# Moving taps, norms and z tiles around the triangular inverse of a gated DeltaNet layer on one core

## The reference, cut to what matters

```python
qkv = jax.nn.silu(causal_depthwise_conv(h[..., Q0:Z0], conv_w))    # 4 taps; q, k, v
q = l2_normalize(qkv[:, :, 0]) * (GDN_HEAD_DIM ** -0.5)
...
a_mat = jnp.where(strict, jnp.einsum('bhncd,bhnsd->bhncs', kb, k) * decay, 0.0)
sol = lax.linalg.triangular_solve(a_mat, rhs, left_side=True, lower=True, unit_diagonal=True)
u, w = sol[..., :Dv], sol[..., Dv:]
qk = jnp.einsum('bhncd,bhnsd->bhncs', q, k) * decay
...
v_new = uc - jnp.einsum('bhcd,bhde->bhce', wc, S)                  # in a scan over the chunks
o = jnp.einsum('bhcd,bhde->bhce', qd, S) + jnp.einsum('bhcs,bhse->bhce', qkc, v_new)
S = S * eg[..., None, None] + jnp.einsum('bhcd,bhce->bhde', kd, v_new)
...
o = o * jax.nn.silu(z)
```

## Time and profile before

| | us |
|---|---|
| median of 3 runs | 2034.25 (2034.21 to 2036.57) |
| profiled execution | 2035.76 |
| its span | 2034.0 |
| TensorE busy | 2009.4 (99%) |
| VectorE busy | 1157.3 (57%) |
| ScalarE busy | 782.3 (38%) |
| mean granted TensorE clock | 0.997 |

### The profile page before, as it was taken

One profiled execution on the slowest core, in us unless ns is written; L12 is line 12 of the kernel. 1 busy time (PEld: TensorE's weight loads), 2 busy tenths in 40 slices (PEclk: granted clock), 3 DMA queues, 4 the chain that ended last, 5 costly groups with the idle time before them and its releaser, 6 DMA issues.

```text
span 2034.0 us, 25396 instructions
## 1 busy us (share of the span) xinstructions
PE 2009.4 (99%) x9637; PEld 1677.9 (82%) x9637; DVE 1157.3 (57%) x1622; ACT 782.3 (38%) x1199; POOL 40.8 (2%) x68
## 2 busy tenths in 40 slices
PE   9999999999999999999999999999999999999998
PEld 7888888878988888888888888888879888888886
DVE  5554532699785755442285545237998766554324
ACT  5222222457765422222252222225586653222223
POOL 1000000011000000000000000000110000000000
PEclk9999999999999999999999999999999999999999
DMA  6333333276222333333323333333761224333331
GB/s 168 113 89 102 95 98 97 73 166 138 60 58 78 104 102 88 99 95 94 101 67 110 93 103 88 102 100 78 174 143 30 54 83 115 95 91 103 116 102 42
DMA packets 332960, 198.50 MB, mean 98 GB/s; under 512 B 9074, under 2 KB 322900, under 8 KB 332884
## 3 DMA queue, kind: packets, MB, share of 16 engines
q1 hardware_dynamic: 327396, 177.55, 30.6%
q0 software_dynamic: 5472, 19.93, 5.3%
q10 hardware_dynamic: 16, 0.00, 0.0%
HBM read 175.43 MB, written 2.10 MB: 87 GB/s over the span
## 4 chain that ended last, share of the span: by engine, by line
PE 84%; DVE 9%; ACT 4%; issue 2%; DMA 0%; SPq 0%; DVEq 0%; ACTq 0%
PE res L562 22%; PE res L564 22%; PE res L563 22%; DVE u L1822 4%; PE res L696 3%; DVE cacc L1904 2%; PE sb L696 1%; PE pq L696 1%; PE res L643 1%; PE res L644 1%; PE res L647 1%; PE pq L924 1%; PE pq L933 1%; PE pq L562 1%; PE pq L564 1%
## 5 line engine op out<-in xcount | busy, mean ns | idle before, releaser
L1134 ACT ACTIVATE wh<-raw 128x1024 fp32r<-128x1024 f32 (+1 forms) x333 | 347.0, 1042 | 991.3 <-PE res L564 906.6
L562 PE MATMUL res<-xh,wh 128*128 128x512 f32 x1560 | 611.6, 392 | 3.7 <-DVE Um L2033 2.6
L564 PE MATMUL res<-xh,wl 128*128 128x512 f32 x1560 | 607.2, 389 | 0.0
L563 PE MATMUL res<-xl,wh 128*128 128x512 f32 x1560 | 607.2, 389 | 0.0
L1640 DVE TENSOR_TENSOR wl<-raw,wh 128x1024 fp32r<-128x1024 f32 (+1 forms) x295 | 354.2, 1201 | 384.9 <-ACT wh L1134 384.9
L562 PEld LDWEIGHTS res<-xh,wh 128*128 128x128 f32 x1560 | 292.9, 188 | 65.1 <-DVE Um L2033 3.1
L564 PEld LDWEIGHTS res<-xh,wl 128*128 128x128 f32 x1560 | 292.8, 188 | 61.7
L563 PEld LDWEIGHTS res<-xl,wh 128*128 128x128 f32 x1560 | 293.0, 188 | 59.9 <-issue 0.5
L562 PE MATMUL res<-hh,wh 128*128 128x512 f32 x528 | 205.4, 389 | 0.0
L563 PE MATMUL res<-hl,wh 128*128 128x512 f32 x528 | 205.4, 389 | 0.0
L564 PE MATMUL res<-hh,wl 128*128 128x512 f32 x528 | 205.4, 389 | 0.0
(11 more groups left out here) (347 smaller groups left out, 2183.9 us busy)
## 6 DMA issues: line engine op xcount, KB each, us to landing
raw<-in_ffn_w_in SPq DMA_DIRECT2D x176, 512.0 KB, 3.9
raw<-in_mix_w_in SPq DMA_DIRECT2D x48, 512.0 KB, 4.0
raw<-in_ffn_w_out SPq DMA_DIRECT2D x46, 512.0 KB, 3.7
raw<-in_ffn_w_out SPq DMA_DIRECT2D x48, 448.0 KB, 3.6
wl<-raw POOLq DMA_DIRECT2D x38, 512.0 KB, 4.9
raw<-in_mix_w_out SPq DMA_DIRECT2D x16, 512.0 KB, 4.0
xin<-in_x SPq DMA_DIRECT2D x8, 256.0 KB, 5.4
out_dram<-xin SPq DMA_DIRECT2D x8, 256.0 KB, 2.2
```

Source lines behind the costliest of these rows:

```text
L562: pe.matmul(bank, wh[:, slot, j, :], hi, start=first, stop=False)
L563: pe.matmul(bank, wh[:, slot, j, :], lo, start=False, stop=False)
L564: return pe.matmul(bank, wl[:, slot, j, :], hi, start=False, stop=last)
L1134: act.activation(wh[:, slot, 0:nk, :], raw[:, slot, 0:nk, :], ACT.Copy).then_inc(hi_full, 1)
```

## The change

Four edits. (1) VectorE makes only the first tap of the last query tile ahead of the four systems, and the other three behind them. (2) ScalarE's activate(11) goes from behind odd_rows(0, 0) to behind turned_u(0, 1), and TensorE's q_norms(3) from the head of level 0 to the head of level 1. (3) The closing turns of head 0 go to the bank pq[0] and those of head 1 to res[0], so that res[1] is free; ScalarE copies each head by an instruction of its own. (4) The two z tiles stand ahead of the wait for u_upd. The same work is done.

```diff
--- before.py
+++ after.py
@@ -341,6 +341,10 @@
 
             return in_bank(head_bank(2 * g, l)) if k == 0 else res[:, 2 * g, :]
 
+        def closing_bank(h):
+
+            return pq[:, 0, :] if h == 0 else res[:, (0, 0, 2, 3)[h], :]
+
         def z_bank(n):
 
             return bc[:, :] if n == 0 else res[:, n % 2, :]
@@ -948,7 +952,7 @@
                         pe.wait_ge(kg_ready, l * H + 2 * g + 1)
                         for j in range(8):
                             h, c = 2 * g + j // 4, j % 4
-                            mm = pe.transpose(res[:, h, c * P:(c + 1) * P], Tm[:, h, c, :], ident[:])
+                            mm = pe.transpose(closing_bank(h)[:, c * P:(c + 1) * P], Tm[:, h, c, :], ident[:])
                     mm.then_inc(tt_full, 1)
 
                 key_products(0)
@@ -974,7 +978,7 @@
                 turn_t(0, 1)
                 p_products(0, 1)
                 for n in range(6):
-                    if n == 0:
+                    if n == 1:
                         q_norms(3).then_inc(q2_full, 1)
                     if n in (1, 2):
                         scores(2 * n - 2)
@@ -1015,8 +1019,8 @@
                     if c == 0:
                         mm.then_inc(vn_full, 1)
 
+                z_tiles(ZT[0])
                 pe.wait_ge(u_upd, l * 14 + 14)
-                z_tiles(ZT[0])
                 own_values(0)
                 w_products(1)
                 for c in range(NC):
@@ -1421,21 +1425,21 @@
                         ins = act.activation(Um[:, 2 * g:2 * g + 2, 0:2, :].rearrange("p h i t -> p h (i t)"),
                                              turn_bank(k, g, l).rearrange("p (h x) -> p h x", h=2), ACT.Copy)
                     else:
-                        ins = act.activation(Um[:, 2 * g:2 * g + 2].rearrange("p h c t -> p h (c t)"),
-                                             res[:, 2 * g:2 * g + 2, :], ACT.Copy)
+                        for h in (2 * g, 2 * g + 1):
+                            ins = act.activation(Um[:, h].rearrange("p c t -> p (c t)"), closing_bank(h), ACT.Copy)
                     ins.then_inc(u_upd, 1)
 
                 turned_first(0)
                 turned_first(1)
                 odd_columns(0, 0)
                 odd_rows(0, 0)
-                activate(3 * H - 1)
                 turned_u(0, 0)
                 turned_first(2)
                 turned_first(3)
                 odd_columns(0, 1)
                 odd_rows(0, 1)
                 turned_u(0, 1)
+                activate(3 * H - 1)
                 odd_rows(1, 0)
                 odd_rows(1, 1)
                 for n in range(6):
@@ -1967,10 +1971,12 @@
 
 
                 qkv_tile(3 * H - 1)
+                qkv_tap(3 * H - 1, 0)
                 for h in range(H):
-                    qkv_tap(3 * H - 1, h)
                     system(h)
                     first_level(h)
+                for k in range(1, GTAPS):
+                    qkv_tap(3 * H - 1, k)
                 dve.wait_ge(br_ready, l + 1)
                 dve.wait_ge(ekd_ready, l + 1)
                 dve.tensor_tensor(gt["kd"][:, 0:16], gt["br"][:, 0:16], gt["ekd"][:, 0:16],
```

## The result

The changed kernel takes 2038.65 us (median of 12 runs, 2037.2 to 2041.06). Twelve runs of the kernel before have a median of 2035.76 us (2034.21 to 2037.18), 1.5 us above the median of three that stood ahead of the prediction. The ratio is 1.0016, with a 95% interval of 1.0009 to 1.0024: 3 us slower. I had forecast 2035.2 us and a range up to 2037.2, a loss of 1.0 us on the three runs that I started from: the sign was right, the size was not, and the time lies outside the range.

A forecast was written before the change was run, and what follows sets the result against it. TensorE, busy 99% of the span, was taken as the bound. Per layer +0.55 us (moved norms) - 0.05 us (z tiles) = +0.5, for two layers +1.0 on 2034.25: 2035.2 us, range 2032.5 to 2037.2.

The forecast's parts named there:

- What bounds the kernel, and the price of a low stretch: TensorE, 99% busy, bounds; some microseconds at 1.2 GHz behind the turn_t(0, 0) wait cost 1.7 us per layer.
- Part 1: VectorE's taps behind the systems: worth 0, since turn_t(0, 0) waits for ScalarE's busy queue; wait stays 1.2 to 1.5 us.
- Part 2: ScalarE's activate(11) behind turned_u(0, 1): price 0, covered by 2.02 us idle before odd_columns(1, 0).
- Part 3: q_norms(3) into level 1: new wait of about 0.5 us before p_products(1, 0), scores(0) 0.55 us later per layer.
- Part 4: Closing turns: another bank and z tiles ahead of the wait let own_values start 1.3 us earlier relative to the turns.
- What is late next: Scan: the 1.3 us become a wait before L1043 of chunk 2 for ScalarE's vn; about 0.05 us gain left.
- Rival A: The scan doesn't hold TensorE back, so 1.3 us stays per layer: 2032.7 us, chance 16%.
- The sum: Both layers: +0.55 - 0.05 = +0.5 us per layer, +1.0 us in all, giving 2035.2 us.
- a stretch more or less in the median run: Allowance in the range 2032.5 to 2037.2 us for one low-clock stretch, costing 1.7 us, more or less.
- The base: Whole kernel: started from the median shown, 2034.25 us, 1.5 us less than the profiled execution's 2035.76.
- Rival D: Level 1: moved norms behind turns and a wait lower the clock again, 1.7 us per layer: 2038.6 us, chance 5%.

The follow-up runs named there:

- e6_early_turn: Kernel before with ScalarE's two mixer_high(Z_U + 3) weight instructions moved from ahead of turned_first(0) to behind activate(11): 2031.05 us, ratio 0.9977.
- e3_taps: Kernel before with the first edit alone, three taps of the last query tile behind the four systems: 2035.88 us, ratio 1.0002.
- e10_level0: Kernel before with taps and activate(11) moved as in the change, but q_norms(3) left at the head of level 0: 2040.84 us, ratio 1.0024.
- e5_tail_scan: Kernel before with edits 3 and 4, plus two convolution taps of scan chunk 1 moved behind VectorE's on: 2034.64 us, ratio 0.9992.
- e13_half: Kernel before with three unneeded 128 x 128 TensorE products ahead of scores(0) in each layer, nothing moved: 2038.88 us, ratio 1.0013.
- e14_first: Kernel before with six unneeded 128 x 128 TensorE products ahead of scores(0) in layer 0 only: 2038.60 us, ratio 1.0014.
- e11_after_mended: Changed kernel plus mixer_high(Z_U + 3) moved later on ScalarE and two scan taps moved behind on: 2028.81 us, six runs, ratio 0.9967 to before.

## Why the prediction was wrong

- **What bounds the kernel, and the price of a low stretch: right.** e6_early_turn won 1.4 and 1.7 us per layer where I had read 1.25 and 1.7.
- **Part 1 (taps, worth 0): right,** by e3_taps, and the reason too, by e6_early_turn. The wait became 1.42 us, within "1.2 to 1.5".
- **Part 2 (activate(11), price 0): right** in that odd_columns(1, 0) was not delayed; e10_level0 shows what it costs if the norms don't follow it.
- **Part 3 (norms, 0.55 us per layer): right in place and kind, a little small.** The wait is 0.35 us, where I had worked out 0.5; scores(0) is 0.55 to 0.69 us later, and another 0.08 us goes before the closing turns. These 0.08 us are in scores(0), whose eight products last 1.14 us behind the norms and 1.06 before.
- **Part 4 and "What is late next": right.** The z tiles start at once and gain 1.49 us (I said 1.3); all of it turns into a wait of 1.1 us before L1047 (I said 1.2). I left 0.05 us as a gain; it is 0.0. Rival A was wrong by the same trace, and e5_tail_scan shows the chain that I had named.
- **The sum: wrong; this is the step that failed.** The result is 3.45 us above the forecast: 1.5 us by the base, 0.4 by part 3, 1.5 by low stretches. I carried the low stretches over as they were: I priced each at 1.7 us, took them as they stood in one profile, and let them change only by a rival with a place in level 1 and by "a stretch more or less in the median run", that is as scatter. So the sum had no term for their number. The change's direct cost is 1.4 us instead of 1.0, and low stretches that come more often add 1.5 us in the mean; e13_half and e14_first show that a mere delay does this. No view of a single profile would have given the term; the spread of the three runs (2034.21, 2034.25, 2036.57) was the hint that the number varies between executions.
- **The base: 1.5 us too low, for the same reason.** I subtracted the 1.5 us between the profiled execution and the median of three. Two of the three were in before's fastest cluster, where 36 of 107 runs are, and twelve runs put the median at the profiled execution's 2035.76. With it the forecast would have been 2036.8, and the range, moved up as a whole to 2034.0 to 2038.7, would just have held the result.
- **Rival D** named 2038.6 us and came closest, by luck: it stood on the low base, and its reason is wrong, since 530 to 534 us in after is at full clock, and the extra stretches lie elsewhere.

What stays open: why a later arrival at the places is worse than that of before, whether their distance or the mere time counts, and whether a larger shift would be better again. e11_after_mended hints that it can go both ways.

## What to carry to other kernels

Before work is taken out of a slack place on a saturated engine and put elsewhere, look at which chain the slack covered: eight narrow products of 0.8 us held up p_products(1, 0) by only 0.2 us in level 0, because VectorE's update was late anyway, and moving them to level 1 cost 0.7 us net. A wait that is filled at the head of a chain is only a gain if the next meeting of the engines has slack too; follow both engines to it in the old trace, where here a weight load that waited 0.2 us told it. And where TensorE drops to its lower clock behind short waits, compare distributions of the granted clock over many runs, not one profile: 1.4 us of direct cost came with 1.5 us of clock. A base from three runs is open to the same error. The gain that held in every trace was to remove the wait that the low stretch comes from.

## What the runs showed of the hardware

TensorE fell to 1.2 GHz behind an idle time of only 1.25 to 1.42 us, where one-column products stood before it and transposes after it; behind the 1.32 us idle time at the closing turns, with full products on its other side, it did not. The same idle time didn't bring the fall each time: in e14_first's layer 0 (1.25 us) the clock stayed at 1.00. Nor is a long idle time needed: at the layers' border in after it was 0.26 us ahead of 1.8 us of one-column products.

A kernel's low stretches are not fixed: the times of the same code lay in three clusters 1.5 us apart in 107 runs, and a delay of 1.3 us in one layer moved the mean by 2.9 us or by 1.4, as the layer was the first or the second. The Trainium skill, "TensorE: Matmul & The Clock Gate", Part 1: The HAM clock gate, "What's actually happening", says of the time until TensorE is first at full clock that one kernel measures different numbers of cold products from run to run, and puts the cost below 1% of a typical kernel's span. Here the number varies in the middle of a kernel too, and four low stretches of 1.7 us are 0.3% of after's span. The runs add that the mean can change by 1.5 us, 0.07% of the span, with the timing of the rest; that is as much as the 1.4 us that this change costs directly.
